# First attention: the later key tiles' softplus added up elementwise, and one product with minus ones in place of up to three

## The reference

```python
z = jnp.einsum('bthd,bshd->bhts', qb, kb).astype(jnp.float32) * scale
strict = s_idx < t_idx
log_not = jnp.where(strict, jax.nn.log_sigmoid(-z), 0.0)
suffix = lax.cumsum(log_not, axis=3, reverse=True) - log_not
a = jnp.where(strict, jnp.exp(jax.nn.log_sigmoid(z) + suffix), 0.0).astype(v.dtype)
outs.append(jnp.einsum('bhts,bshd->bthd', a, vb))
```

## Time and profile before

| | us |
|---|---|
| median of 3 runs | 1454.19 (1452.59 to 1454.44) |
| profiled execution, its own time | 1454.88 |
| its span in the profile | 1453.1 |
| TensorE busy | 1436.5 (99%) |
| TensorE weight loads | 1195.4 (82%) |
| VectorE busy | 874.8 (60%) |
| ScalarE busy | 634.7 (44%) |
| GpSimd busy | 390.4 (27%) |

### The profile page before, as it was taken

One profiled execution on the slowest core, in us unless ns is written; L12 is line 12 of the kernel. 1 busy time (PEld: TensorE's weight loads), 2 busy tenths in 40 slices (PEclk: granted clock), 3 DMA queues, 4 the chain that ended last, 5 costly groups with the idle time before them and its releaser, 6 DMA issues.

```text
span 1453.1 us, 18674 instructions
## 1 busy us (share of the span) xinstructions
PE 1436.5 (99%) x7320; PEld 1195.4 (82%) x7320; DVE 874.8 (60%) x1309; ACT 634.7 (44%) x1047; POOL 390.4 (27%) x327
## 2 busy tenths in 40 slices
PE   9999999999999999999999999999999999999998
PEld 7777778888888888888888878888889888888887
DVE  6455666444576644565447436788757877348754
ACT  6545772232453321444345336555545444234442
POOL 1363220102032200121014412115525452334512
PEclk9999999999999999999999999999999999999999
DMA  8351116545264545357427212134613234213341
GB/s 275 114 174 59 59 44 229 205 160 165 88 229 144 172 143 175 116 195 227 139 94 264 74 58 74 59 117 147 228 60 116 87 103 136 97 59 92 98 131 58
DMA packets 54913, 191.19 MB, mean 132 GB/s; under 512 B 6759, under 2 KB 7688, under 8 KB 54442
## 3 DMA queue, kind: packets, MB, share of 16 engines
q1 hardware_dynamic: 48314, 167.06, 35.6%
q0 software_dynamic: 4880, 17.30, 3.6%
q10 hardware_dynamic: 1632, 5.64, 1.0%
HBM read 177.38 MB, written 12.60 MB: 131 GB/s over the span
## 4 chain that ended last, share of the span: by engine, by line
PE 82%; DVE 7%; ACT 4%; POOL 3%; DMA 3%; issue 2%; ACTq 0%; POOLq 0%; DVEq 0%
PE PS L597 80%; DMA raw<-in_ws 2%; PE PS L610 2%; DVE TMP L2748 1%; DVE wl L2088 1%; DVE wl L2085 1%; ACT wh L1398 1%; POOL wl L2857 1%; ACT wh L1393 1%; POOL s1w L3081 1%; POOL TMP L3083 1%; POOL FFl L3053 1%; DVE TMP L2135 0%; ACT Y L1412 0%; ACT th L1977 0%
## 5 line engine op out<-in xcount | busy, mean ns | idle before, releaser
L2085 DVE TENSOR_TENSOR wl<-raw,wh 128x1024 fp32r<-128x1024 f32 x193 | 256.7, 1334 | 268.2 <-ACT wh L1398 267.6
L597 PE MATMUL PS<-HTh,wh 128*128 128x512 f32 (+1 forms) x1052 | 394.6, 376 | 3.4 <-DVE wl L2085 2.2
L597 PE MATMUL PS<-HTl,wh 128*128 128x512 f32 (+1 forms) x1052 | 391.1, 373 | 0.0
L597 PE MATMUL PS<-HTh,wl 128*128 128x512 f32 (+1 forms) x1052 | 387.1, 373 | 0.0
L1398 ACT ACTIVATE wh<-raw 128x1024 fp32r<-128x1024 f32 x210 | 220.1, 1054 | 196.9 <-PE PS L597 177.6
L597 PEld LDWEIGHTS PS<-HTh,wh 128*128 128x128 f32 x1052 | 198.7, 189 | 45.1 <-issue 8.2
L597 PEld LDWEIGHTS PS<-HTh,wl 128*128 128x128 f32 x1052 | 196.3, 189 | 35.8 <-DVE wl L2085 0.2
L597 PEld LDWEIGHTS PS<-HTl,wh 128*128 128x128 f32 x1052 | 198.6, 189 | 32.9 <-DVE HTl L2103 0.6
L597 PE MATMUL PS<-wl,FFh 128*128 128x512 f32 (+1 forms) x442 | 169.9, 384 | 0.0
L597 PE MATMUL PS<-wh,FFh 128*128 128x512 f32 (+1 forms) x442 | 169.9, 384 | 0.0
L597 PE MATMUL PS<-wh,FFl 128*128 128x512 f32 (+1 forms) x442 | 169.8, 384 | 0.0
(11 more groups left out here) (366 smaller groups left out, 2440.8 us busy)
## 6 DMA issues: line engine op xcount, KB each, us to landing
raw<-in_ws SPq DMA_DIRECT2D x268, 512.0 KB, 4.3
taps<-TMP SPq DMA_DIRECT2D x16, 256.0 KB, 2.4
tab<-in_spec POOLq DMA_DIRECT2D x8, 512.0 KB, 5.7
raw<-taps SPq DMA_DIRECT2D x8, 512.0 KB, 3.8
kd<-TMP POOLq DMA_DIRECT2D x16, 256.0 KB, 6.6
wh<-in_wd POOLq DMA_DIRECT2D x8, 512.0 KB, 4.1
wl<-in_wd POOLq DMA_DIRECT2D x8, 512.0 KB, 5.5
kf<-kd SPq DMA_DIRECT2D x8, 512.0 KB, 4.5
```

The lines of the kernel that those rows point to most:

```text
L597: return nc.tensor.matmul(out, l, r, start=start, stop=stop, skip_group_check=True)
L2085: tt(l, RAW[RAW_AT["unit", x, 0] % RAWS][:, :UNITS[x][2]], f32(h), ALU.subtract).then_inc(sem("lo_dve"), 1)
```

## The change

After the change the columns of `SPH` and `SPL` that belong to key tile 2 and query tile 3 are overwritten, once step 0's products are done, by the split of the sum of key tiles 3 and 2; after step 1, tile 1's columns for query tiles 2 and 3 by the split of the sums over key tiles 1 to 3. So each step needs the products for the next key tile j = s + 1 only. Three parts:

- GpSimd makes the sums in f32 (`later_sums`), right after the two `affine_select` of a step: two adds and two copies (128 columns each) in step 0, four adds in step 1, none in step 2, into new buffers `RF1` and `RF0`.
- VectorE splits them (`later_split(p)`), as the first thing in its loop's step p, after TensorE's products of step p: a cast and a subtraction for each of two heads, of 128 columns in step 0 and 256 in step 1.
- TensorE's `later_keys` in steps 1 and 2 does one pair of products for j = s + 1 and waits for that head's split first. ScalarE's Abs, which overwrites the TMP buffer, waits for the sums too.

```diff
           "g_side": (("dec0", 1), ("tap_ed", 16), ("pg", 17), ("mx_gu", 2), ("t_sum", 4)),
-          "g_sum": (("eg_add", 2), ("g_add", 12), ("w_sum", 36)),
+          "g_sum": (("sb_r", 32), ("eg_add", 2), ("g_add", 12), ("w_sum", 36)),
...
+        RF1, RF0 = at("rf1", 175, [P, 2, P]), at("rf0", 203, [P, 2, 256])
...
+        def SUMMED(n, last):
+            c, step = divmod(n // 2, 3)
+            return 8 * c + 4 * step + 2 * (n % 2) + last
+        def SPLIT(n):
+            c, step = divmod(n // 2, 3)
+            return 4 * c + 2 * step + n % 2 + 1
...
-                for j in range(3, s, -1):
-                    c = LEFT(s) + P * (j - s)
-                    o = slice(OFF[j], OFF[j] + S - P * j)
-                    mm(PS[:, b, c:w], NEG[:, 1, :], SPH[h % 2][:, o], False, False)
-                    mm(PS[:, b, c:w], NEG[:, 1, :], SPL[h % 2][:, o], False, True)
+                j = s + 1
+                c = LEFT(s) + P
+                o = slice(OFF[j], OFF[j] + S - P * j)
+                if s < 2:
+                    e.wait_ge("sb_rl", SPLIT(n - 2))
+                mm(PS[:, b, c:w], NEG[:, 1, :], SPH[h % 2][:, o], False, False)
+                mm(PS[:, b, c:w], NEG[:, 1, :], SPL[h % 2][:, o], False, True)
...
                 e.wait_ge("sb_pl", n - 2)
+                if n >= 3 and (n - 3) // 2 % 3 < 2:
+                    e.wait_ge("sb_r", SUMMED(n - 3, 2))
...
+            def later_split(p):
+                h, ss = SB[2 * p]
+                if ss[-1] == 0:
+                    return
+                for i in range(2):
+                    n = 2 * p + i
+                    x, o = (RF1[:, i, :], slice(256, 384)) if ss[-1] == 2 else (RF0[:, i, :], slice(512, 768))
+                    e.wait_ge("p_lk", n + 1)
+                    e.wait_ge("sb_r", SUMMED(n, 1) if ss[-1] == 2 else SUMMED(n, 2))
+                    nc.vector.tensor_copy(SPH[i][:, o], x).then_inc(sem("sb_rh"), 1)
+                    e.wait_ge("sb_rh", SPLIT(n))
+                    tt(SPL[i][:, o], x, f32(SPH[i][:, o]), ALU.subtract).then_inc(sem("sb_rl"), 1)
...
             for p in range(PAIRS + 1):
+                if p < PAIRS:
+                    later_split(p)
...
+            def later_sums(n):
+                step, x, r1, r0 = n // 2 % 3, T(n % 3), RF1[:, n % 2, :], RF0[:, n % 2, :]
+                if step == 2:
+                    return
+                e.wait_ge("sb_k", n + 1)
+                if step == 0:
+                    e.wait_ge("p_mix", 4)
+                    e.wait_ge("sb_rl", SPLIT(n - 4) if n >= 6 else 0)
+                    tt(r1, x[:, 256:384], x[:, 0:128], ALU.add).then_inc(sem("sb_r"), 1)
+                    nc.gpsimd.tensor_copy(r0[:, 0:128], x[:, 128:256]).then_inc(sem("sb_r"), 1)
+                else:
+                    e.wait_ge("sb_r", SUMMED(n - 2, 2))
+                    tt(r0[:, 0:128], x[:, 128:256], r0[:, 0:128], ALU.add).then_inc(sem("sb_r"), 1)
+                    tt(r0[:, 128:256], x[:, 256:384], r1, ALU.add).then_inc(sem("sb_r"), 1)
...
             def keep_scores(p):
...
+                for n in (2 * p, 2 * p + 1):
+                    later_sums(n)
```

More of the change, by code:

```diff
@@ L288 @@
           "v_weight": (("sb_pl", 24), ("df_w", 16)),
-          "v_narrow": (("ff_sq", 32), ("uc_v", 154), ("fin_y", 3)),
-          "v_wide": (("o_y", 8), ("fo_y", 16), ("o2_v", 8), ("dn_v", 17)),
+          "v_narrow": (("sb_rl", 16), ("ff_sq", 32), ("uc_v", 154), ("fin_y", 3)),
+          "v_wide": (("sb_rh", 16), ("o_y", 8), ("fo_y", 16), ("o2_v", 8), ("dn_v", 17)),
           "v_x": (("x2", 4), ("x1", 4), ("fin", 4)),
```

## The result

The changed kernel took 1463.89 us (median of 6 runs, 1462.69 to 1464.71), the kernel before 1452.76 (6 runs, 1451.24 to 1454.44): ratio 1.0070, interval 1.0060 to 1.0081. It is slower by 11.1 us in the medians and lies outside the predicted range (1456.3 to 1462.8). The profiled executions, 1463.94 and 1454.88 us, are 9.1 apart; the one of before was among its slower ones, so all that follows from the two traces is about that 9.1.

What follows compares the result with a forecast made beforehand. TensorE, busy 1436.5 of 1453.1 us, was taken to bound the kernel. Waits and savings of +4.4 us and one clock fall of +1.6 made +6.0, on the median of 1454.19 a forecast of 1460.2 us, range 1456.3 to 1462.8.

Steps and rivals of the forecast that it cites:

- the port: GpSimd's new sums hold up VectorE's casts beside them: 0.2 to 0.3 us for each pair of steps 0 and 1.
- What goes: Products removed from TensorE in steps 1 and 2, 16 pairs of 128 columns and 8 of 256: 5.0 us saved.
- Place A: Step 1 of the first head pair: TensorE stands 3.4 us for the first split, lateness +2.5.
- Place B: Step 2 of the first head pair: TensorE waits 0.25 us, saves 0.92, lateness +1.8.
- Place C: The two middle heads: step 2 waits of about 1.05 us against savings, about -0.1 in all, lateness +1.7.
- Place D: The last head: VectorE has little idle time, TensorE stands about 3.7 us, lateness +4.4.
- The clock: Stands of 3.4 and 3.7 us in the first and last heads lower TensorE's granted clock: one fall taken, 1.6 us.
- Rival 3: Pairs with sums each lose 0.6 to 0.9 us of VectorE's time: +7 to +9, 1461.5 to 1463 us, chance 0.09.
- Rival 1: The kernel is late, but TensorE's clock stays up: +4.4, 1458.6 us, chance 0.20.
- rival 2: Saving and new waits cancel, small splits and sums at lower bounds: +1 to +2.5, 1455.2 to 1456.7 us, chance 0.16.
- rival 4: Faster, because splits are ready before TensorE comes: 1450 to 1451 us, chance 0.06.

Runs made afterwards that it cites:

- e3: Changed kernel with matmuls that nobody reads filling TensorE's two long stands (n = 2 and n = 22): 1460.36 us, ratio 1.0049 to before.
- e1: Changed kernel with only the removal of products kept, no sums, splits or waits on them (output incomplete): 1449.22 us, ratio 0.9974 to before.
- e7: The change applied in the two middle heads only, first and last as in the kernel before: 1453.09 us, ratio 1.0000 to before.
- e2: Changed kernel without GpSimd's sums or waits for them; the splits read a constant: 1457.53 us, ratio 1.0028 to before.
- e8: The change in the middle heads only, each split moved between the two softplus parts of VectorE's next step: 1451.83 us, ratio 0.9993 to before.
- e12: As e8, but only step 2 uses a sum; step 1 keeps its products and has no split: 1450.79 us, ratio 0.9983 to before.
- e9: Changed kernel with the last head put back as in the kernel before: 1457.18 us, ratio 1.0028 to before.
- e10: Changed kernel with GpSimd's sums kept, but the splits read a constant and wait for no sum: 1462.95 us, ratio 1.0070 to before.
- e6: Changed kernel with the first head's step 0 split moved ahead of VectorE's softplus of n = 2: 1459.95 us, ratio 1.0050 to before.
- e13: Changed kernel with the first head pair's four step 0 sums moved behind GpSimd's two gate-and-up products: 1463.11 us, ratio 1.0065 to before.
- e4: Changed kernel with splits sent to a scratch buffer and TensorE not waiting for them (output incomplete): 1459.76 us, ratio 1.0049 to before.
- e11: Changed kernel, all heads: first split ahead of the softplus of n = 2, others between the next step's two softplus parts: 1456.26 us, ratio 1.0018 to before.
- e5: Kernel before plus 32 VectorE instructions of the splits' sizes into a scratch buffer, no sums, all products kept: 1454.95 us, ratio 1.0015 to before.
- e14: e12 extended to the first head, whose first sums stand behind the gate-and-up products: 1451.25 us, ratio 0.9989 to before.

## Why the prediction was wrong

The direction and the mechanism held, the size did not: +11.1 us where +6.0 was forecast. In the traces it is 9.1, of which 6.5 are waits less savings (e3, the clock up) where 4.4 was forecast, and 2.7 the clock where 1.6 was. The steps that failed are two terms of the sum: the hold that the sums put on VectorE ("the port", 0.2 to 0.3 us), the larger one, and the single fall of the clock. By the prediction's steps:

1. **What goes** (-5.0): right. e1 has -4.0, with 1.1 us in waits that no step of mine had.
2. **Place A**: the wait was 3.99 us for 3.4, the lateness without the clock 3.1 for 2.5 (e3). The GpSimd queue (0.8 us) came as worked out. The missing part is the hold: `OTl` +0.26, the split +0.34, the cast ahead of it 0.61 for 0.54, less the 0.2 that I had taken.
3. **Place B**: TensorE did not wait at all, for 0.25, but only because the slow clock had made it late. In e3 it waits 0.36 us there.
4. **Place C**: with the clock up the two heads took the lateness from 2.6 to 3.3 (e3), +0.7 for my -0.1. Alone (e7) they cost 0.3.
5. **Place D**: a stand of 3.74 us for 3.7, and part of this agreement is luck. The products ahead of the stand start at 207.50 us against 202.24, 5.1 us late where I had 1.7, and a wait of 0.81 at step 1 stands ahead that I had not listed. My own numbers give 208.6 - 203.04 - 1.7 = 3.9 us for the stand, not 3.7. Without the clock the last head added 3.2 us (3.3 to 6.5) for my 2.7.
6. **The port**, the larger mis-sized term: 0.2 to 0.3 was taken where place A lost 0.7. Over the four heads the 128-column splits alone lost 8 x 0.23 on the casts and 8 x 0.11 on the subtractions, 2.7 us of VectorE's time. What the sums cost TensorE is an estimate from e3 less e2, with the slow work behind e2's two stands (1.4 and 1.5 us in its trace) taken out: 1.4 us at A, 0.4 at B, 1.3 at C and 0.8 at D, 3.9 in all and less if e2's falls were partly taken back. Of it the queue is 0.8 at most. The rule that the prediction cited (the Trainium skill, "SBUF — State Buffer", section "Who interferes with whom") put 1.5 us on top for the subtractions. The trace agrees with the rule in kind: 398 ns for a subtraction with the sums in the kernel, 292 without, but that is 0.11 us more in the mean and not a whole sum. The cast is held too, 448 for 216, and a cast has one input; the same section allows that for copies and casts in its two-port modes.
7. **The clock**: one fall of 1.6 us was taken, two came, at both stands. The slow work was 2.0 and 1.4 us; the net price is 2.7 us in the lateness of after against e3 and 3.5 in the medians. That a fall at A is partly lost in later waits and one at D is not was right: 1.2 of A's 2.0 us were left behind the middle heads. What failed is the count. The prediction knew the two stands, had a row in which 2.33 us ended in a fall, and still counted one.
8. **The level**: the medians are 11.1 us apart and the traces 9.1, and no term had the other 2.0. The six executions of before have a median 1.4 us under the three that I had, and the profiled one, 1454.88, lay 2.1 above it. The fall behind the 2.33 us stand does not explain it by itself: the changed kernel's trace has the same stand (2.32 us) and the same granted clock behind it (0.60 from 880 to 884 us), so it cancels in the 9.1. Whether before has this fall in fewer of its executions is not shown.

Rival 3 (the port decides, 1461.5 to 1463, chance 0.09) came nearest. Its loss of 0.6 to 0.9 us a pair was there in the four pairs of step 0 (2 x 0.34 us in the splits) and not in those of step 1, and it too had one fall. Rival 1 (the clock stays up) is refuted by the windows, rival 2 by all of A and D, rival 4 by the sign; its condition, splits that are ready in time, was met by e8 and e12 in the two heads where it can be.

Not settled: where the 2.0 us between traces and medians come from; why e9's median is 2 us better than its theory; what separates a wait of 1.5 us that ends in a fall (e9 and e10 at 172 us) from one that does not (the changed kernel, e3, e6, e7, e13 at the same place); and how e4's 7 us divide between the clock, the sums and the waits in VectorE's queue.

## What to carry to other kernels

Price each long stand of TensorE (here 2.5 to 4.0 us) at its length and a fall of the clock behind it, two stands at two falls, unless the record shows such a stand without one. Then ask which later wait takes part of the fall back (here 0.8 of 2.0 us at A, nothing at D). Work that is put on a slack engine is not free: ask what stands behind it in that engine's queue (here the next split, which TensorE needs anyway), and what its accesses hold up on the engine beside it. Before giving up such a change, apply it only where the slack is (here two of four heads) and only where it saves much for each microsecond of the second engine (0.92 for 1.5 us at step 2, against 0.34 for 1.0 at step 1).

## What the runs showed of the hardware

- Two small elementwise operations, one on GpSimd and one on VectorE, stretch each other, in the worst rows about twofold: casts of 128 columns 448 ns for 216, subtractions 398 for 292, sums on GpSimd 0.76 to 0.90 us for 0.46. Once a copy of 128 columns on GpSimd, 0.29 or 0.42 us elsewhere, took 1.29:

```profile
178.80 1.29 POOL L2975 COPY rf<-TMP 128x128 f32<-128x128 f32 x1
```

- It can also go well: the cast of n = 1 that took 1.43 us beside GpSimd's 512-column product took 0.61 in the changed kernel, where small sums stood in the product's place, and 1.43 again in e13.
- A fall of the clock followed every stand of TensorE of 2.5 us and more in this stretch (the changed kernel, e2, e6 at D, e9, e10, e13), and also pairs of shorter ones (1.23 and 1.74 us in e11, 0.41 and 1.33 and again 1.88 and 1.13 in e4) and a single one of 1.5 us in e9 and e10, but not in five other traces. Filled with matmuls of no use, the same stands had none (e3). The fall near 872 us is there in the traces of before, the changed kernel, e1, e2, e4, e5, e7, e9, e11 and e14 and missing in those of e3, e6, e8, e10, e12 and e13, all with the same work there.
